# Moving the A logits of the cached sequences into the rounds, and the B cache row copies and late probabilities one place on

## The reference

```
h = rmsnorm(x, g_pre)
[qA kA vA fA zA | qB kB vB zB | gA gB] = h @ w_in              # w_in is 1024 x 7176
A (8 heads x 64): softmax(q k / 8 + C[t] - C[s]) v,  C = cumsum(log sigmoid(fA + b_f))
   cached sequence: 4 pages x 128 positions from a page pool, and its new token
B (3 groups x 4 heads x 64): keys at distances 0, d, 2d, .. up to the window,
   (window, d) = (128, 1), (512, 4), (2048, 16); bias by distance; the groups combined by weight
   cached sequence: window buffers b0, b1, b2; returned shifted by one row, new row at the end
u = sigmoid(gA) * ((oA * silu(zA)) @ w_br_a) + sigmoid(gB) * ((oB * silu(zB)) @ w_br_b)
x = x + rmsnorm(u @ w_out, g_post)
x = x + sigmoid(x @ w_ple_gate) * rmsnorm(p @ w_ple, g_ple)
```

## Time and profile before

| | |
|---|---|
| runs | 664.72, 666.17, 668.34 us, median 666.17 |
| profiled execution | 667.82 us, its span from first to last instruction 666.0 us |
| TensorE busy | 602.6 us (90%), mean granted clock 0.968 |
| VectorE, ScalarE, GpSimd busy | 363.5, 242.1, 137.4 us |
| DMA | 100.50 MB, mean 151 GB/s |

### The profile page before, as it was taken

How to read it: one execution, slowest core, us unless ns; L and a number is a source line. 1 busy time by engine, 2 the same in 40 slices (tenths; PEclk the granted TensorE clock), 3 DMA queues, 4 the chain that set the end, 5 groups by cost and what they waited for, 6 DMA issues and landing times.

```text
span 666.0 us, 12810 instructions
## 1 busy us (share of the span) xinstructions
PE 602.6 (90%) x4890; PEld 566.3 (85%) x4890; DVE 363.5 (55%) x878; ACT 242.1 (36%) x549; POOL 137.4 (21%) x155
## 2 busy tenths in 40 slices
PE   3999979999999999999899778999699969999893
PEld 2989979999999999899799778886479959999893
DVE  2766355556445555545766676432127845588842
ACT  6744233435344434334222125222103375444210
POOL 3014010110100300000667885011003242000000
PEclk9999979999999999999999988999869999999997
DMA  9439782644622682322299995577612165212111
GB/s 248 106 98 351 236 265 64 222 127 128 198 64 72 172 302 84 109 66 68 76 294 296 301 325 147 168 229 217 192 57 64 32 194 170 65 32 65 48 49 34
DMA packets 106203, 100.50 MB, mean 151 GB/s; under 512 B 6523, under 2 KB 93871, under 8 KB 105856
## 3 DMA queue, kind: packets, MB, share of 16 engines
q1 hardware_dynamic: 102528, 73.69, 38.3%
q0 software_dynamic: 3568, 25.99, 11.2%
q10 hardware_dynamic: 48, 0.01, 0.0%
HBM read 92.37 MB, written 26.12 MB: 178 GB/s over the span
## 4 chain that ended last, share of the span: by engine, by line
PE 65%; DMA 11%; DVE 7%; issue 5%; ACT 4%; SPq 4%; POOL 3%; DVEq 0%; POOLq 0%; ACTq 0%
PE pj L824 40%; DMA w_raw<-in_w_in_dram 5%; PE tr L824 5%; PE tr L816 5%; PE sc L918 3%; PE pv L947 3%; DMA qbc<-q_dram 2%; POOL prod L680 1%; PE sc L824 1%; SPq L507 1%; ACT w_hi L1145 1%; POOL prod L684 1%; DMA w_raw<-in_w_out_dram 1%; SPq L509 1%; DMA kv_b<-in_cache_b_kv_dram 1%
## 5 line engine op out<-in xcount | busy, mean ns | idle before, releaser
L824 PE MATMUL pj<-h_hi,w_hi 128*128 128x256 f32 (+1 forms) x960 | 284.4, 296 | 10.3 <-ACT gsig L1169 10.3
L824 PE MATMUL pj<-h_lo,w_hi 128*128 128x256 f32 (+1 forms) x960 | 273.8, 285 | 0.0
L824 PE MATMUL pj<-h_hi,w_lo 128*128 128x256 f32 (+1 forms) x960 | 273.3, 285 | 0.0
L824 PEld LDWEIGHTS pj<-h_hi,w_hi 128*128 128x128 f32 x960 | 184.0, 192 | 15.0 <-issue 13.4
L824 PEld LDWEIGHTS pj<-h_lo,w_hi 128*128 128x128 f32 x960 | 183.9, 192 | 0.0
L824 PEld LDWEIGHTS pj<-h_hi,w_lo 128*128 128x128 f32 x960 | 183.4, 191 | 0.0
L1401 DVE TENSOR_TENSOR w_lo<-w_raw,w_hi 128x1024 fp32r<-128x1024 f32 (+2 forms) x84 | 96.2, 1148 | 59.7 <-ACT w_hi L1145 59.7
L1145 ACT ACTIVATE w_hi<-w_raw 128x1024 fp32r<-128x1024 f32 (+2 forms) x84 | 81.7, 974 | 100.1 <-DMA w_raw<-in_w_in_dram 41.3
L1408 DVE COPY probT<-tr 128x256 f32<-128x256 f32 (+3 forms) x56 | 27.3, 488 | 50.9 <-PE tr L816 50.9
L680 POOL TENSOR_TENSOR prod<-kv_a,qbc 128x512 f32<-128x512 f32 x24 | 36.2, 1536 | 15.8 <-DMA kv_b<-in_cache_b_kv_dram 10.7
L824 PE MATMUL tr<-h_hi,w_hi 128*128 128x256 f32 (+1 forms) x128 | 37.0, 289 | 0.5 <-issue 0.5
(11 more groups left out here) (364 smaller groups left out, 962.6 us busy)
## 6 DMA issues: line engine op xcount, KB each, us to landing
w_raw<-in_w_in_dram SPq DMA_DIRECT2D x52, 512.0 KB, 5.1
kv_a<-in_cache_a_kv_dram SPq DMA_DIRECT2D x64, 256.0 KB, 3.5
out_dram<-in_cache_b_kv_dram POOLq DMA_DIRECT2D x16, 1022.0 KB, 10.9
qbc<-q_dram SPq DMA_DIRECT2D x8, 640.0 KB, 5.5
kv_b<-in_cache_b_kv_dram SPq DMA_DIRECT2D x32, 128.0 KB, 3.1
w_raw<-in_w_out_dram SPq DMA_DIRECT2D x8, 512.0 KB, 4.4
w_raw<-in_w_ple_gate_dram SPq DMA_DIRECT2D x8, 512.0 KB, 4.1
x_in<-in_x_prompt_dram SPq DMA_DIRECT2D x4, 512.0 KB, 6.5
```

The source lines that it names most:

```text
L824: ins = nc.tensor.matmul(out, w[:, k0, :], x[:, c_x, lo:hi], start=first and i == 0, stop=last and i == 2)
```

## The change

1. The A logits of the cached sequences are made in rounds 6 to 9, two sequences per round. Queries of the new tokens for A are known after round 3; in round 4 they are transposed (`qa_tok`), written to DRAM by GpSimd (`qa_dram`), and SyncE asks for their broadcast and the four pages of keys behind the weight loads of the rounds (`keys_a`; its hardware loop over rounds is written out). GpSimd makes all 32 products (`prod_r`, three buffers), VectorE the 32 reductions (`logits_a`), one in each of the loops i = 3 to 10.
2. The stage of the gate tiles keeps the B logits alone: a query of 768 values per row, three slices, three products. Two sequences share a tile (t = 1 to 4) and a weight load. The softmax comes at t = 6, the probabilities at t = 8, the value sums at t = 9 to 16, one sequence per tile.
3. In the two-unit rounds 7 to 10 (`late`) `probs_t`, `values` and their counterparts on the other engines come one loop later, and in round 10 the combination of the groups at i = 5 instead of 4.
4. Copies: b0 in round 1, one sequence of b1 in each of rounds 2 to 9; the eight copies of b2 in the branch tiles, one ahead of each `h_lo` on GpSimd (that loop is written out).
5. The transpositions of `x_in` and `xs_in` go from rounds 7 and 8 to rounds 0 to 4 (`RAW_AT`). On VectorE the copy of such a group and `qk_lo` stand ahead of `evac1` and `lo_part`. The rearrangement of round 5's first B group through DRAM (`o0_dram` and its readback) is split over rounds 7 and 8.

The core of the diff:

```diff
+PRODS, RPRODS = 8, 3
+R_QA, R_LOGITS = ROUNDS_A, ROUNDS_A + 2
+RAW_AT = {0: {11: 0}, 1: {9: 1, 11: 2}, 2: {9: 3, 11: 4}, 3: {9: 5, 11: 6}, 4: {11: 7}}
+T_ROWS, T_PROBS, T_VALUES = 6, 8, 9
...
@@ SyncE
+            def keys_a(s):
+                if s == 0:
+                    sp.wait_ge(S["s_qad"], 16)
+                    sp.wait_ge(s_pt, 16)
+                if s >= 2:
+                    sp.wait_ge(S["s_prod"], PAGES * (s - 1))
+                sp.dma_start(qbc_r[s % 2][:, :], qa_dram[s:s + 1, :].to_broadcast([P, AW])).then_inc(S[f"s_qb{s % 2}"], 16)
+                pages(s, 0, kv_r)
+            for r in range(ROUNDS_A + 1, ROUNDS + 1):
+                for j in range(3):
+                    load(3 * r + j)
+                    if r > R_LOGITS and j < 2:
+                        keys_a(2 * (r - 1 - R_LOGITS) + j)
...
             for s in range(DEC):
                 sample_queries(s)
                 if s:
-                    sample_rows(s, 0)
+                    slices(s, 0, kv_k)
+                if s % 2:
+                    load(n)
+                    n += 1
...
@@ GpSimd, rounds
+                if r == 1:
+                    copy_rows(0, 0, DEC)
+                elif r < ROUNDS:
+                    copy_rows(1, r - 2, r - 1)
...
+                if r >= R_LOGITS and r < ROUNDS:
+                    for s in (2 * (r - R_LOGITS), 2 * (r - R_LOGITS) + 1):
+                        pool.wait_ge(S[f"s_qb{s % 2}"], 16 * (s // 2 + 1))
+                        pool.wait_ge(S[f"s_kp{s % 2}"], 64 * (s // 2 + 1))
+                        for p in range(PAGES):
+                            k = PAGES * s + p
+                            if k >= RPRODS:
+                                pool.wait_ge(S["s_red"], k - RPRODS + 1)
+                            nc.gpsimd.tensor_tensor(prod_r[k % RPRODS][:, :], kv_r[s % 2][:, p, :], qbc_r[s % 2][:, :], ALU.mult).then_inc(S["s_prod"], 1)
...
@@ GpSimd, output
-            with pool.Fori(0, DC) as m:
+            for m in range(DC):
+                copy_rows(2, m, m + 1)
                 pool.wait_ge(S["s_mh"], m + 1)
...
@@ TensorE
-                    if 1 <= i <= nu:
-                        probs_t(r, i - 1)
+                    late = nu == 2
+                    if 1 <= i - late <= nu:
+                        probs_t(r, i - late - 1)
...
-                if 13 <= t < 17:
-                    sample_values(pe, t - 13)
-                if t >= 17:
-                    sample_values(pe, 2 * t - 30)
-                    sample_values(pe, 2 * t - 29)
+                if T_VALUES <= t < T_VALUES + DEC:
+                    sample_values(pe, t - T_VALUES)
...
@@ VectorE
+            def logits_a(k):
+                dve.wait_ge(S["s_prod"], k + 1)
+                V.tensor_reduce(lg_a[:, k % PAGES, k // PAGES, :], prod_r[k % RPRODS][:, :].rearrange("p (h d) -> p h d", d=HD), AX.X, ALU.add).then_inc(S["s_red"], 1)
...
+                    if r >= R_LOGITS and r < ROUNDS and 3 <= i < 11:
+                        logits_a(PAGES * 2 * (r - R_LOGITS) + i - 3)
...
+                if 1 <= t < 5:
+                    sample_logits(2 * t - 2)
+                    sample_logits(2 * t - 1)
```

More of the change, by code:

```diff
@@ L242, in build @@
         cursor[0] = after_g
+        qa_tok = sb("qa_tok", [DEC, AW], at=at_g)
+        kv_r = [sb(f"kv_r{i}", [P, PAGES, AW], at=at_g + 4 * 3 * T if i == 0 else None) for i in range(2)]
+        qbc_r = [sb(f"qbc_r{i}", [P, AW]) for i in range(2)]
+        prod_r = [sb(f"prod_r{i}", [P, AW]) for i in range(RPRODS)]
+        assert cursor[0] <= after_g
+        cursor[0] = after_g
         at_2 = cursor[0]
@@ L489, in _, with pages, slices @@
                     load(3 * r + 5)
[L490 to L494, removed]
+            def pages(s, kv, bufs):
+                for p in range(PAGES):
+                    page = sp.value_load(pt[0:1, PAGES * s + p:PAGES * s + p + 1], min_val=0, max_val=POOL_PAGES - 1)
+                    src = A["cache_a_kv"][0, bass.ds(page, 1), :, kv, :, :].rearrange("o t h d -> (o t) (h d)")
+                    sp.dma_start(bufs[s % 2][:, p, :], src).then_inc(S[f"s_kp{s % 2}"], 16)
+            def slices(s, kv, bufs):
+                for g in range(BG):
+                    n, step = SLOTS[g], DIL[g]
+                    src = caches[g][0, s, 0:n * step:step, kv, :, :].rearrange("t h d -> t (h d)")
+                    sp.dma_start(bufs[s % 2][0:n, g, :], src).then_inc(S[f"s_bk{s % 2}"], 16)
+            def keys_a(s):
[11 more added lines that the diff above has]
+                        keys_a(2 * (r - 1 - R_LOGITS) + j)
+            for n in range(TILE_G + 3, TILE_G + 7):
                 load(n)
@@ L537, in _ @@
             sp.dma_start(sm[0:DEC * BH, 1:1 + BG], selfb_dram.rearrange("s (h g) -> (s h) g", g=BG)).then_inc(S["s_selfr"], 16)
-            sample_rows(0, 1)
-            load(n + 3)
-            sample_rows(1, 1)
-            load(n + 4)
-            load(n + 5)
-            n += 6
+            for s in range(2):
+                load(n)
+                n += 1
+                pages(s, 1, kv_a)
+                slices(s, 1, kv_b)
+            for k in range(T_VALUES - 6):
+                load(n)
+                n += 1
             for s in range(2, DEC):
+                load(n)
+                n += 1
                 sp.wait_ge(S["s_samp"], s - 1)
-                sample_rows(s, 1)
+                pages(s, 1, kv_a)
+                slices(s, 1, kv_b)
+            for k in range(3):
                 load(n)
@@ L1294, in _ @@
                         evac0(n)
-                    if 2 <= i <= nu + 1:
-                        values_out(r, i - 2)
-                    if r == ROUNDS and i == 4:
+                    late = nu == 2
+                    if 2 <= i - late <= nu + 1:
+                        values_out(r, i - late - 2)
+                    if r == ROUNDS and i == 5:
                         act.wait_ge(S["s_md"], 1)
@@ L1615, in _ @@
                         V.tensor_copy(later[:, :], pv[0][:, 0:PAGES * DEC * AH]).then_inc(S["s_lsum"], 1)
-                    if 1 <= i <= nu:
-                        probs_out(r, i - 1)
+                    late = nu == 2
+                    if 1 <= i - late <= nu:
+                        probs_out(r, i - late - 1)
+                    if i in RAW_AT.get(r, ()):
+                        out_of_turn((xT[:, RAW_AT[r][i], 0:SEQ], lambda b: b[:, :]))
+                    if r < ROUNDS and i in (5, 9):
+                        qk_lo(r, i // 4 - 1)
                     if i % 4 == 3:
```

166 lines of the change are left out of this document (66 added, 100 removed).

## The result

The changed kernel takes 644.78 us (median of 4 runs, 642.24 to 645.71) against 665.87 for the kernel before, a ratio of 0.966 with an interval of 0.964 to 0.969. Two later sets of six runs gave 642.97 (ratio 0.967, 0.962 to 0.973) and 646.73 (0.975, 0.969 to 0.981). The forecast was 634.7 in a range of 624 to 650. The profiled execution took 642.24 us with a span of 640.1, so by the trace 25.9 us of span are gone, where the sum had 31.5.

The account below looks back on a forecast made before the run. TensorE, working 602.6 of 666.0 us, was taken as the bound. From 667.8, gains 25.9, 6.3 and 4.8 less costs 1, 1, 0.5 and 3 gave 636.3; less 1.65 for the median, 634.7 us, range 624 to 650.

Parts of the forecast that it names:

- the likeliest case: The forecast itself, 634.7 us with its own range 628 to 641, given a chance of 0.68.
- Round 2: Fewer copies ahead of round 2 let its weight load land in time: 31.20 to 24.9 us, 6.3 us gained.
- Probabilities one slot on: Rounds 7 to 10: one more group of products covers TensorE's wait for exponentials, 4.8 us gained, bounds 0 and 4.8.
- Logits in the rounds: Rounds 6 to 9: added products and reductions mostly covered by VectorE's idle, cost 1 us, bounds 0 and 27.
- The gate stage: Gate tiles through first output tile: without A logits, 141.2 us against 167.06, 25.9 us gained.
- the pair cycle: Gate tiles: queries, slices and products take 7.5 us per pair of sequences, delaying weight loads; cost 1 us, bounds 0 and 7.2.
- Rival 3: The pair cycle of 7.5 us governs the first gate tiles: 7.2 us instead of 1, so 641 us; chance 0.05.
- the end: Last two plain gate tiles at 5.76 us each and first output tile at full clock, 10.4 us.
- Copies in the output stage: Eight copies among the output tiles delay about one link of the load chain: cost 3 us, bounds 0 and 13.
- Rivals 1 and 4: Output stage: copies hold it, 13 us instead of 3, 645, chance 0.12; chained late loads, 43 instead of 3, 675, chance 0.03.
- Their sign: Output stage: ScalarE waiting for branch, `w_ple` or `w_out` loads by more than 5 us in all.
- From the trace to the median: Whole kernel: median taken 1.65 us below the profiled execution, turning 636.3 into 634.7 us.

Follow-up runs that it names:

- the copies alone on before: Kernel before the change with only the copies moved (b0 in round 1, one b1 in each of rounds 2 to 9, b2 in the branch tiles): 663.07 us, ratio 0.988.
- fills: Changed kernel with each GpSimd product of rounds 6 to 9 replaced by a zero fill of the same buffer, leaving out the cached sequences' A logits: 639.18 us.
- the one-buffer kernel: Changed kernel with one buffer instead of three for GpSimd's products in the rounds: 680.42 us.
- The earlier load: Changed kernel with one weight load of the gate tiles, and so each later one, asked for one pair of sequences earlier: 641.01 us.
- copies as before: Changed kernel with the old copy placement (b0, b1, b2 in round 1, b1 and b2 in each of rounds 2 to 8, none in the branch tiles): 652.32 us.

## Why the prediction was right or wrong

Direction and order of size were right, and 644.78 lies in the range, but outside the likeliest case's own 628 to 641, in which 0.68 of the chance lay. By its steps:

- **Round 2** (6.3 forecast): 35.36 to 29.76 us, 5.6; the raw transposes that moved in took 0.7. Shown by the copies alone on before (29.02). The load that took 30.2 us to land takes 19.3 in the changed kernel, more than the half that the prediction took, and still came in time.
- **Probabilities one slot on** (4.8): the four waits of 1.2 us came back when it was undone, 5.2 us by the medians.
- **Start of the kernel** (no term): 1.8 us, by no mechanism that the sum has.
- **Logits in the rounds** (1, bounds 0 and 27): rounds 7 to 9 are 1.2 to 2.1 us longer in all than with fills. Reductions wait for products 0.6 us in all, where the prediction wanted under 0.5. The reason given was incomplete: the prediction weighed a rule of the Trainium skill (SBUF — State Buffer, Who interferes with whom) and let the 0.25 us per product speak against it. That 0.25 is a mean over 17 products that were not held up and seven that were, by up to 2 us. The differences of 1.42 us beside products and 0.68 beside fills agree with the rule, and the fills with what the same section adds, that a GpSimd instruction which only writes SBUF does not contend. The price was small only because most of it fell into VectorE's idle. Upper bound 27: the one-buffer kernel lost 34 to 37, of which 20 us are TensorE's idle in rounds 6 to 9; the bound left out the clock.
- **The gate stage** (25.9 less 1 for the pair cycle): 18.6. This is the step that failed, by 6.3 us, and it was mis-sized in two terms. First the pair cycle, taken as 1 of 7.2 us: cycle (7.7 us between loads) and place were right, the slack was counted too high; 2.34 us of idle and 1.7 us of low clock, and in all 51.57 us up to the first transposition of the probabilities against 48.1 in the sum (8 x 5.76, one of the 2 us of transposes, and the softmax's 1). Rival 3, at 0.05, was half true: ScalarE waited up to 6.3 us for a load, where the prediction wanted none over 2. The earlier load took 3.1 to 4.0 us out of this stretch. Second the end, 25.60 us against 21.9 (2 x 5.76 and 10.4). With no value sums behind the last two tiles, TensorE waits three times, as these rows of the changed kernel show (in brackets the idle):

```profile
450.64 0.36 PE L855 MATMUL pj<-h_hi,w_hi 128*128 128x256 f32 x1 [1.03 <-DVE zsil L1539]
457.57 1.44 PE L815 MATMUL pv<-st,d_a 8*32 8x512 f32 x3 [0.98 <-issue]
465.54 0.59 PE L855 MATMUL pj<-og_hi,w_hi 128*128 128x264 f32 x1 [1.19 <-DVE og_lo L1784]
```

  The first two waits are new. The first is the z tile's own chain; the second the profile puts down as issue, but VectorE's `zsil` of the last z tile starts at 457.05 us, in the middle of it, so it is most likely the same chain. The third stood in the kernel before as well (1.19 us, at 494.06). The sum named that chain and gave it 1 us once; idle is 3.20 us in all. It also took the first output tile at full clock, and behind the third wait the clock is 0.61 for 3.8 us, which is 1.5 us. No run tried this end by itself. The eight tiles with sums came as computed, 64.22 against 64.1 (8 x 7.89 and the other 1 of the transposes), at a clock of 1.00.
- **Copies in the output stage** (3, bounds 0 and 13): 2.7, but the number is right by luck. There was no chain of late loads: idle is 20.8 us as before, one small load came later, and the clock behind it was lower. From the last branch product to the end the traces take 136.0 to 139.3 us with copies and 135.3 to 136.1 without. From the first branch product on they take 179.0 to 182.6 and 178.9 to 181.5, so that the net price is about 1 us and not clear of the scatter; the branch tiles' own clock goes from 0.85 to 0.96 with copies and from 0.86 to 0.92 without, and what sets it no run shows. Rivals 1 and 4 did not come by their price. Their sign, waits of more than 5 us for branch, `w_ple` or `w_out` loads, did (6.6 us), but the kernel before has 5.0 of them already, so it was set too low.
- **From the trace to the median**: the sum took 1.65 us off, since before's profiled run lay that much above the median. The changed kernel's lay 2.5 below its own, at a mean granted clock of 0.981 where the three other runs have 0.973 to 0.976: 4.2 us of the miss of 10.1 are this, and why those runs had the lower clock no trace shows.

## What to carry to other kernels

When work that stood between two tiles goes away, look for the chain that it hid and price every place where it comes out, not one. A load queue needs its deadline worked out link by link: ask for what the busiest engine needs ahead of requests that wait for a product. Price a stall with what the clock may lose behind it: 1.98 us of idle cost 3 us more here, though other stalls of that length cost nothing more. A mean duration that is 0.25 us high can hide a few instructions that are held up for 2 us: look at the longest before speaking against a rule.

## What the runs showed of the hardware

- A VectorE difference of two SBUF inputs (128x512) took 1.42 us beside a GpSimd product and 0.68 beside a GpSimd fill; w_lo up to 2.36 for 1.23. The reductions, of one input, stayed at 0.67 to 0.68 us in both.
- GpSimd's product of 128x512 takes 1.29 us by itself; the mean of 1536 ns in the earlier trace rows holds seven of 24 that were held up, to 3.26 us at most. The profile counts the time in which either engine was held up as busy time.
- After one idle of 1.98 us (at the end of round 8, copies as before) the granted clock was 0.87 over the next 26 us, 0.50 between 276 and 282 us, with no idle over 0.4 in it. After 0.71 us (at the end of round 8 of the changed kernel) it stayed at 1.00, and so it did after 2.40 us ahead of the `w_ple` tile without copies, over the next 10 us; after 3.77 us there, with copies, it was 0.83 over these.
- A load of 128 KB landed after 3.6 us beside one copy of 1 MB between DRAM regions and after 2.2 us without; one of 512 KB after 30.2 us beside copies of 6 MB, 19.3 beside 3 MB.
